# A chunked delta-rule recurrence on one NeuronCore: eight block lanes of one PSUM bank each, Gram products over 64 rows, an unrounded correction matrix and a 64x64 state update

## What the reference computes

```python
def step(S, inp):
    r_t, w_t, k_t, v_t, a_t, b_t = inp          # decay w, keys k, values v, a = -kk, b = kk * a
    sa = jnp.einsum('bhij,bhj->bhi', S, a_t)
    S = (S * w_t[:, :, None, :] + sa[..., None] * b_t[:, :, None, :]
         + v_t[..., None] * k_t[:, :, None, :])
    return S, jnp.einsum('bhij,bhj->bhi', S, r_t)
S0 = jnp.zeros((bsz, N_HEADS, HEAD_DIM, HEAD_DIM), f32)
_, y = lax.scan(step, S0, seq)
```

## Time and profile before

| | |
|---|---|
| median of three runs | 3082.04 us (3081.85 to 3089.59) |
| the profiled execution | 3081.99 us, its span in the trace 3080.2 us |
| TensorE (PE) busy | 2978.4 us, 97% of the span |
| VectorE (DVE), ScalarE (ACT), GpSimd (POOL) busy | 1819.8, 1312.4, 520.9 us |
| the recurrence, first to last matmul | about 256 to 575 us of the span |

### The profile page before, as it was taken

The page is one execution under the profiler, slowest core; times in us unless marked ns, Lnnn a source line. Parts: engine busy times, 40 slices in busy tenths (PEclk is TensorE's granted clock), DMA queues, the critical chain, the costliest instruction groups (busy, mean ns, idle before and its releaser), DMA issues.

```text
span 3080.2 us, 46647 instructions
## 1 busy us (share of the span) xinstructions
PE 2978.4 (97%) x19342; PEld 2598.9 (84%) x19342; DVE 1819.8 (59%) x2676; ACT 1312.4 (43%) x2276; POOL 520.9 (17%) x464
## 2 busy tenths in 40 slices
PE   6999999999999999999999999998999999999999
PEld 6986666799999999999999987667888878878887
DVE  7676555548768553555867856664544543365353
ACT  4465666433223355663323445553323332243232
POOL 0002323123113100002312323001211201112020
PEclk9999999999999999999999999999999999999999
DMA  3210000025545322003554531102322322223222
GB/s 105 80 52 35 1 2 1 36 102 179 179 159 185 123 94 68 1 35 138 183 181 164 196 123 55 42 1 69 96 96 89 99 86 90 95 76 104 91 91 91
DMA packets 79555, 284.33 MB, mean 92 GB/s; under 512 B 8528, under 2 KB 9296, under 8 KB 78576
## 3 DMA queue, kind: packets, MB, share of 16 engines
q1 hardware_dynamic: 79344, 281.35, 27.5%
HBM read 274.96 MB, written 6.36 MB: 91 GB/s over the span
## 4 chain that ended last, share of the span: by engine, by line
PE 90%; DVE 5%; ACT 3%; issue 1%; POOL 0%; DMA 0%; DVEq 0%; SPq 0%; ACTq 0%; POOLq 0%
PE psum L348 65%; PE psum L2675 2%; PE psum L889 2%; PE psum L1836 2%; PE psum L2047 2%; PE psum L1247 2%; PE psum L2029 1%; PE psum L2020 1%; ACT XH L1360 1%; PE psum L832 1%; PE psum L1270 1%; PE psum L529 1%; PE psum L2372 1%; DVE xt L732 1%; PE psum L2669 1%
## 5 line engine op out<-in xcount | busy, mean ns | idle before, releaser
L303 DVE TENSOR_TENSOR wlo<-wraw,whi 128x1024 fp32r<-128x1024 f32 (+2 forms) x398 | 508.3, 1298 | 629.2 <-ACT whi L296 627.7
L296 ACT CAST whi<-wraw 128x1024 fp32r<-128x1024 f32 (+2 forms) x398 | 396.4, 1022 | 514.4 <-PE psum L348 482.7
L431 DVE CUSTOM_DVE_ANT_0 araw<-araw,cond 128x1024 f32<-128x1024 f32 x112 | 181.1, 1655 | 0.0
L348 PE MATMUL psum<-f0xh,whi 128*128 128x264 f32 x704 | 143.7, 286 | 4.9 <-DVE f0xl L574 3.3
L348 PE MATMUL psum<-f1xh,whi 128*128 128x258 f32 x704 | 142.5, 284 | 4.8 <-DVE f1xl L574 3.3
L348 PE MATMUL psum<-f2xh,whi 128*128 128x512 f32 x352 | 140.3, 399 | 3.5 <-DVE f2xl L570 3.5
L348 PE MATMUL psum<-f3xh,whi 128*128 128x512 f32 x352 | 140.3, 398 | 3.5 <-DVE f3xl L570 3.5
L348 PE MATMUL psum<-f0xh,wlo 128*128 128x264 f32 x704 | 143.5, 285 | 0.0
L348 PE MATMUL psum<-f0xl,whi 128*128 128x264 f32 x704 | 143.1, 285 | 0.0
L348 PE MATMUL psum<-f1xh,wlo 128*128 128x258 f32 x704 | 142.5, 284 | 0.0
L348 PE MATMUL psum<-f1xl,whi 128*128 128x258 f32 x704 | 142.0, 283 | 0.0
(11 more groups left out here) (532 smaller groups left out, 8414.4 us busy)
## 6 DMA issues: line engine op xcount, KB each, us to landing
wraw<-d_w SPq DMA_DIRECT2D x357, 512.0 KB, 3.4
araw<-d_ada SPq DMA_DIRECT2D x112, 512.0 KB, 3.3
wraw<-d_w SPq DMA_DIRECT2D x32, 384.0 KB, 3.4
hn<-d_h SPq DMA_DIRECT2D x4, 528.0 KB, 7.4
hres<-d_h SPq DMA_DIRECT2D x1, 2112.0 KB, 8.2
spill<-hres SPq DMA_DIRECT2D x1, 2112.0 KB, 7.4
hres<-spill SPq DMA_DIRECT2D x1, 2112.0 KB, 8.5
cond<-d_cond SPq DMA_DIRECT2D x2, 1024.0 KB, 4.9
```

What stands on the lines that cost most here:

```text
L296: e.copy(whi[0:rows, n % NH, 0:kt * cols], wraw[0:rows, n % NR, 0:kt * cols]).then_inc(*w_hi.up(n))
L303: e.tensor_tensor(wlo[0:rows, n % NH, 0:kt * cols], wraw[0:rows, n % NR, 0:kt * cols], whi[0:rows, n % NH, 0:kt * cols].bitcast(F32), ALU. ...
L348: ins = e.matmul(psum[0:bw, b0 + nb * len(sl) + si, 0:ln], l_ if z == 2 else h_, (xp.lo if z == 1 else xp.hi)[:, k, o:o + ln], start=k == ...
L431: e.tensor_tensor_reduce(out=w, in0=w, in1=self.c[:, col, :], scale=1.0, scalar=0.0, op0=ALU.mult, op1=ALU.add, accum_out=ada[:, ly, blk, ...
```

## The change

- Eight lanes, one for each block, issued as four pairs with five turns between pairs; each block has one PSUM bank. A pair's step issues both blocks' instructions one after the other. All blocks go through the chunks once.
- `tr` and `zp` are replaced by `g0` (BT) and `g1` (KT). Each issues, for a pair, four fp32 matmuls of 64 rows and 256 columns, alternately on rows 0 to 63 and 64 to 127 and into the pair's two banks. ZP, its clearing and its copies are gone.
- `z1` is issued in step `x1`, with a wait for all masks of the pair. A full chunk has 19 steps.
- `s2` is two fp32 matmuls with A unrounded; AR and AL are gone.
- The transposes of BT and KT are issued in `s3`, in full chunks only, and one 128x384 copy brings out U and both.
- The state is 64 columns wide in PSUM: four fp32 matmuls of 64x64 output (two of keys and values, two of B and U). GpSimd scales the old state by the decay; VectorE adds the scaled product in two operations of 64x64.
- The rounding copy of Z1 moves from ScalarE to VectorE. The tile `selc` lies elsewhere.

The core of the diff:

```diff
-        NLN = 4
-        AR = mem.left("AR", [128, NLN, 2, 128], F32R)
-        AL = mem.left("AL", [128, NLN, 2, 128], F32R)
+        SKEW = 5
+        _steps = [(c, s) for c in range(5) for s in lane_steps(c)]
+        SCAN = [(p, *_steps[_t - SKEW * p]) for _t in range(len(_steps) + 3 * SKEW) for p in range(4)
+                if 0 <= _t - SKEW * p < len(_steps)]
+        ONES = [(blk, c, s) for p, c, s in SCAN for blk in (2 * p, 2 * p + 1)]
...
-                    for w, src in enumerate((BT, KT)):
-                        ins = e.matmul((p1, p0)[w].rearrange("p (a t) -> p a t", a=4)[:, :, 0:T], src[:, blk, q.tok],
-                                       q.Zp[:, :, 0:T], start=True, stop=True)
+                    w = int(s[1])
+                    if w:
+                        e.wait_ge(*c_gm.at(two[1].blk, c, 0, 1))
+                    elif c:
+                        e.wait_ge(*c_S.at(two[1].blk, c - 1, 1))
+                    for l, q in enumerate(two):
+                        for j in range(2):
+                            rows = slice(64 * j, 64 * j + 64)
+                            ins = e.matmul(q.pg[:, j, l, :, 0:q.T], (BT, KT)[w][rows, q.blk, q.tok], RA[rows, :, q.blk, q.tok],
+                                           start=True, stop=True)
...
+                    if s == "x1":
+                        e.wait_ge(*c_ai.at(blk, c, 1))
+                        e.wait_ge(*c_gm.at(two[1].blk, c, 1, 1))
...
-                        e.matmul(o, q.Ar[0:T, j, 0:T], w1, start=f, stop=False, skip_group_check=True)
-                        ins = e.matmul(o, q.Al[0:T, j, 0:T], w1, start=False, stop=True, skip_group_check=True)
+                            ins = e.matmul(q.p[:, 128 + 64 * j:192 + 64 * j], q.A[0:T, j, 0:T], q.Wr[0:T, 0, 64 * j:64 * j + 64].bitcast(F32),
+                                           start=True, stop=True)
...
+                        if c < 4:
+                            for w, src in enumerate((BT, KT)):
+                                e.transpose(q.p[:, 128 + 128 * w:256 + 128 * w], src[:, blk, q.tok], ident)
...
-                        e.matmul(b, q.tB[0:T, 1, :], vtok[0:T, c, 128 * blk:128 * blk + 128], start=True, stop=False)
-                        e.matmul(b, q.tB[0:T, 0, :], q.U[0:T, :], start=False, stop=True).then_inc(*c_sm.up(blk, c))
+                                e.matmul(st[64 * j:64 * j + 64, :], q.tB[0:T, 1, 64 * j:64 * j + 64], vtok[0:T, c, 64 * h:64 * h + 64],
+                                         start=False, stop=False, skip_group_check=True)
...
+                                ins = e.matmul(st[64 * j:64 * j + 64, :], q.tB[0:T, 0, 64 * j:64 * j + 64], q.U[0:T, 64 * j:64 * j + 64],
+                                               start=False, stop=True, skip_group_check=True)
```

More of the change, by code:

```diff
@@ L1196, in program, with __init__ @@
         c_ye = sig("c_ye", at("y"))
-        c_sm = sig("c_sm", [x for x in at("y") if x[1] < 4])
+        c_sf = sig("c_sf", [x for x in at("y") if x[1] < 4])
         c_S = sig("c_S", [(*x, i) for x in at("y") if x[1] < 4 for i in range(2)])
[L1200 to L1205, removed]
         class Lane:
-            def __init__(self, ln, blk, c):
+            def __init__(self, blk, c):
+                self.blk, self.c = blk, c
                 self.T = T = 128 if c < 4 else 16
-                self.t0, self.NL = 128 * c, 7 if c < 4 else 4
-                self.A, self.Ar, self.Al, self.Ak = AA[:, ln], AR[:, ln], AL[:, ln], AK[:, ln]
-                self.X, self.W, self.Zp, self.R, self.tB, self.S = XX[:, ln], WW[:, ln], ZP[:, ln], RBK[:, ln], tokB[:, ln], St[:, ln]
-                self.Z1, self.U = self.A[:, 0, :], self.A[:, 1, :]
-                self.Ah, self.Xh, self.Wh = AH[:, ln], XH[:, ln], WH[:, ln]
-                self.b0, self.b1 = 2 * ln, 2 * ln + 1
+                self.NL = 7 if c < 4 else 4
+                self.A, self.Ak, self.R, self.S = ZA[:, blk, 1:3], AK[:, blk], RBK[:, blk], St[:, blk]
+                self.Ah, self.Xh, self.Wh = AH[:, blk], XH[:, blk], WH[:, blk]
+                self.Zr, self.X, self.Wr = Zr[:, blk], XT[:, blk], WR[:, blk]
+                self.Z1, self.U, self.tB, self.UB = ZA[:, blk, 0], ZA[:, blk, 0], ZA[:, blk, 1:3], ZA[:, blk]
+                self.p, self.pf = psum[0:T, blk, :], psum[:, blk, :]
+                pair = blk - blk % 2
+                self.pg = psum[0:T, pair:pair + 2, :].rearrange("p j (l a t) -> p j l a t", l=2, a=2)
+                self.gr = self.pg[:, :, blk % 2]
+                self.px = self.p.rearrange("p (j x) -> p j x", j=4)
                 self.bc = lambda m: m[0:T, 0:T].unsqueeze(1).broadcast_to((T, 2, T))
@@ L1226, in scan_pe @@
         def scan_pe(e):
[L1227 to L1232 removed]
+            for pr, c, s in SCAN:
+                two = [Lane(blk, c) for blk in (2 * pr, 2 * pr + 1)]
+                if s in ("g0", "g1"):
+                    w = int(s[1])
[3 more added lines that the diff above has]
+                        e.wait_ge(*c_S.at(two[1].blk, c - 1, 1))
@@ new lines, in scan_dve @@
+            e.wait_ge(*p_sb.at(4))
+            for blk, c, s in ONES:
+                q, T = Lane(blk, c), (128 if c < 4 else 16)
+                if s in ("g0", "g1"):
+                    w = int(s[1])
+                    if not (w or c):
+                        e.memset(q.S[:, :], 0.0).then_inc(*c_S0.up(blk))
+                    e.wait_ge(*c_g.at(blk // 2, c, w))
+                    e.tensor_tensor((q.A, q.Ak)[w][0:T, :, 0:T], q.gr[:, :, 0, 0:T], q.bc(mU),
+                                    ALU.mult).then_inc(*c_gm.up(blk, c, w, 0))
+                    e.tensor_tensor(q.R[0:T, 2 * w:2 * w + 2, 0:T], q.gr[:, :, 1, 0:T], q.bc(mUI),
+                                    ALU.mult).then_inc(*c_gm.up(blk, c, w, 1))
@@ new lines, in scan_dve @@
+                    e.wait_ge(*c_ye.at(blk, c))
+                    for j in range(2):
+                        own = slice(64 * j, 64 * j + 64)
+                        e.scalar_tensor_tensor(out=q.S[own, own], in0=q.pf[own, 256:320], scalar=Fc[own, blk, c:c + 1],
+                                               in1=q.S[own, own], op0=ALU.mult, op1=ALU.add).then_inc(*c_S.up(blk, c, j))
+        def scan_pool(e):
+            for blk, c, s in ONES:
+                q, T = Lane(blk, c), (128 if c < 4 else 16)
+                if s == "g0":
```

331 lines of the change are left out of this document (128 added, 203 removed).

## The result

The changed kernel takes 3045.02 us (median; before, measured beside it, 3084.24). The ratio is 0.9865, 95% interval 0.985 to 0.9881: 1.35% faster, and 1 us from the forecast of 3046. The recurrence was forecast at 283 us and lasts 278.5. But two of its parts are far from what I wrote, in opposite directions: the full rounds are 23 us shorter than forecast, the two ends 19 us longer. The execution profiled with the result was in a slow state (3638.69 us, mean clock 0.73), so all rows "after" are those of the same kernel in the experiment `a_again` (profiled at 3041.9 us, span 3040.1).

A forecast was written before the change was run, and what follows sets the result against it. TensorE (PE) was taken to bound the recurrence, 318.8 us. PE work of 6.9 plus waits of 0.85 gave 7.75 us a block; 32 x 7.75 + 35 = 283 us, 35.8 less, so 3046 us, range 3018 to 3070.

The forecast's parts named there:

- Gram products: TensorE's Gram matmuls on row halves: 1.2 us a block against 1.66 before, ends 0.83 and 1.66.
- no overlap: Rival: Gram row halves don't run side by side, Gram 1.66, 8.36 us a block, 3069 us; chance 0.15.
- drains: Rival: PE empties at each switch between full rows and halves, 0.4 us a block, 3059 us; chance 0.08.
- s2: Correction with A unrounded on PE: four records in 0.4 us a block against 0.59, at worst no gain.
- The state and y: PE's y step with the 64x64 state products: 1.51 us a block, no gain and no loss.
- s3, x1, z1, W and X: Other PE steps, us a block: s3 0.39 + 0.29 for the transposes, x1 with z1 0.84, W and X 2.04.
- Waits: PE's waits in a full round, for masks and the new state: 0.85 us a block against 1.03 before.
- one bank for a lane: Rival: a turn lasts as long as its longest matmul, mask and copy chain, 9.25 us a block, 3094 us; chance 0.05.
- The round: A full round of eight blocks in the recurrence: 8 x 7.75 = 62 us.
- full overlap: Rival: Gram halves run side by side (0.83), eight blocks hide nearly all waits, 6.93 us a block, 3018 us; chance 0.20.
- Start and small chunks: The recurrence's two ends: 10 us start, 18 to 22 small chunks, 5 drain; 35 against 44.2, bounds 30 and 42.

The follow-up runs named there:

- a_again: The changed kernel run again unchanged, for a profile at the full granted clock: 3043.12 us, ratio 0.987.
- a_wide_state: The changed kernel with the state's products 128x128 again, two fp32 matmuls in place of four of 64x64 for a block: 3060.28 us, ratio 0.9929.
- a_two_pairs: The changed kernel with two pairs at work instead of four, four blocks in flight, the second pair nine turns behind: 3133.86 us, ratio 1.0166.
- the fillers: The changed kernel with 72 unused fp16 matmuls of 512 columns added, 35 in turns 1 to 9 and 37 in the last: 3050.02 us, ratio 0.9884.

## Why the prediction was right, and where two errors met

**The bound and the place.** PE was the limit of the stage and all of the change's effect lies in the stage: confirmed, 40.3 us less there, 40 in the span.

**Gram products.** Taken at 1.2 between 0.83 and 1.66, measured 1.06. The row halves overlap; what the 0.23 us above full overlap are, no run shows. The rival "no overlap" falls. The rival "drains" falls in its size: it had 0.4 us a block for the switches of the Gram steps, and the whole Gram work is only 0.23 over pure streaming.

**s2** 0.4, measured 0.445: right. In the kernel before, between other neighbours, the same form took 0.50 to 0.60 and gave nothing.

**The state and y.** The mechanism holds, a size was off: 1.51 forecast, 1.22 measured. I had priced the state's eight records like L1313's (0.074 of 128 columns); they have 64 columns, and eight of them took 0.11 + 0.22 = 0.33 and not 0.59. a_wide_state shows it in the kernel's time (17 us). The Trainium skill, TensorEngine Tiling (Array Packing), section Instruction Overhead, says that a matmul of one column takes as long as one of 60 and that no tiling factor should be taken from a dimension that is already small. The prediction worked out from this that the small products would cost as much each as the wide ones. That goes further than the rule: they have 64 columns, so they lie just above its 60. The trace disagrees with what was worked out, 0.33 against 0.75 (0.55 in the kernel before, where no half-width matmul stood between them). The Trainium skill, TensorEngine Tiling (Array Packing), section Key Properties, says that a change of the tiling mode drains the engine. Of such a drain the traces here have at most 0.1 to 0.15 us for a change from half to full width, and less than 0.1 the other way.

**s3, x1, z1, W and X** came out at 0.50, 0.78 and 1.90 where I had 0.68, 0.84 and 2.04: two blocks' instructions of one kind now stand together; that this is the reason was not tested. The sum is 6.14 and not 6.9.

**Waits**: 0.85 forecast, 7.03 - 6.14 = 0.89 measured. g1's wait of 0.6 to 0.8 a pair was 0.91 in the trace above; y to g0 0.40 a pair, as taken. The one at x1 is 0.32. The rival "one bank for a lane" foresaw 9.25 us a block from chains that aren't covered: with four blocks in flight that is what happens (9.1, a_two_pairs, with GpSimd in the chain beside the masks), with eight it isn't.

**The round**: 62 forecast, 56.2 measured, -5.8 in each of four rounds, 23 us in all. This alone would have put the kernel at 3023, near the rival "full overlap" (3018), whose 6.93 a block is the nearer of the two.

**The step that failed is "Start and small chunks"**: 35 us forecast with 42 as its bound, 53.7 measured (278.5 - 4 x 56.2). The start costs 15 and not 10: with five turns between pairs, PE has one pair for five turns and two for five, and those run at 1.2 GHz. Three turns bring it to 9.2. Small chunks and drain cost 39 and not 23 to 27, so the larger part of the miss, about 14 us, is here. PE is busy 35.3 of the last 37.6 us, at a clock of 0.55. In this stretch y with the state takes 2.2 us a block and not 1.2:

```profile
514.37 0.80 PE L1307 MATMUL psum<-RA,St 128*128 128x128 f32 x2
...
516.58 0.80 PE L1307 MATMUL psum<-RA,St 128*128 128x128 f32 x2
```

PE's idle time there is only 2.3 us, which speaks for the clock and against the waits in the chain of a pair's thirteen steps. No run sets the two apart: the fillers didn't lift the clock there. I had allowed for a slow clock in before's figure (17.5 for a round of small chunks, in which some 7 us were at 1.2 GHz), but not for a longer stretch of small matmuls at the lower clock, some 34 us, after they were all put in one place.

The forecast of the total was therefore right to 1 us by two errors of about 20 us. The range of 3018 to 3070 holds the time; the single number is right by luck. Two sums in the prediction are off without changing this: a Gram of 1.6 and a tail of 42 come to 3066 together and not to the 3058 given, and the one-bank rival's 6.9 and 2.4 make 9.3, 3096 us.

## What to carry to other kernels

Smaller arithmetic in a pipeline of lanes pays only if what stands between two of TensorE's steps (here four masks of VectorE) is covered: measure the parts alone and then with more lanes. Here two parts gave nothing alone and all three gave nothing together, and with the lanes the kernel was 1.3% faster. When a schedule is made wider, price its two ends by themselves, with the clock that TensorE gets there, and try the distance between lanes as a number: here three turns beat five by 0.6% (half of it seen in the stage), and two were as slow as five. Take a term from the row with the same shape in all dimensions, the streamed columns too; the state's term was wrong because a row of twice the columns stood in for it.

## What the hardware showed that I had not expected

- fp32 matmuls on rows 0 to 63 and 64 to 127 of the array run side by side, whichever order they are issued in (four matmuls of 256 columns in 1.06 us; two of 128 rows and 512 columns in 1.66).
- Four fp32 records (two matmuls) of 64x64 output with 64 columns take 0.11 us when half-width matmuls follow, 0.22 when a full-width one does.
- TensorE can be 99% busy and at 1.2 GHz: late in the stage, where chunks of 16 tokens are among the work, the granted clock is 0.50 although PE is busy 9.90 of 10 us:

```profile
510.00:520.00 10.00, 9.90 (x85) 8.77 (x85) 1.73 (x8) 2.31 (x10) 1.21 (x2) 0.50 0.01 2
```

- 35 wide fp16 matmuls among the first ten turns keep the clock at 1.00 there; 37 of them in the last turns don't.
